# A layer stack on one core: the input ratio joined to the output matrix, state-space preparation dealt out anew, and a feed-forward entry with an early split and no wait at the barrier

## The chip, the cores and the metric

The kernel runs on one core of a Trainium2 chip. The core has TensorE (PE, matrix products into PSUM), VectorE (DVE), ScalarE (ACT), GpSimd (POOL) and SyncE (SP, which here only issues DMAs). The metric is the device time of one launch, in microseconds; the kernel before has a median of 1590.62 us over 3 runs.

## The reference

Three layers over 256 tokens of width 1024, all in float32. What matters here is the end of the first mixer, the feed-forward after it, and the mixer of the second layer:

```python
h = gdn_mixer(...)                                   # layer 0: gated delta rule, ends in o @ w_out
x = layer_norm(ALPHA * x + h, ln_g[0, 0], ln_b[0, 0])
f = (silu(x @ w1) * (x @ w3)) @ w2                   # D_FF = 2816
x = layer_norm(ALPHA * x + f, ln_g[0, 1], ln_b[0, 1])
# layer 1: s5_mixer, a diagonal complex state-space model, 64 groups of 16 channels and 64 states
u = x @ w_in
a_bar = exp(lam * dt)
b_bar = ((a_bar - 1.0) / lam)[..., None] * (b_re + 1j * b_im)
h_t = a_bar * h_(t-1) + einsum('gpc,tgc->tgp', b_bar, u_t)
y_t = einsum('gcp,tgp->tgc', c_re + 1j * c_im, h_t).real
# ... skip, gelu, gated output, layer norm, a mixture of experts; then a second block
# (convolution and gating mixer, a hierarchical mixture of experts, an embedding gate, a norm)
```

The factor (a_bar - 1) / lam is what is called the ratio below. It depends on group and state, not on time or channel.

## The kernel before

The program is one stream per engine, written out by hand, with counting semaphores between the streams. The weights go through a ring of three units of 16 KB per partition (`ring`); SyncE loads unit u once unit u - 3 is `released`.

**Split products.** A float32 product is made of three passes in a rounded type (`fp32r`): ScalarE rounds a weight piece of 128 x 1024 into a buffer (the high part), VectorE subtracts it from the ring in place (the low part), and TensorE runs high x high, low x high and high x low. The activations have a high part (`xT_r`) and a low part (`xl`) too.

**Feed-forward** (`ffn_tensor`, `ffn_scalar`, `ffn_vector`). The 22 chunks of hidden width are handled in blocks of 4, 4, 3, 4, 4, 3. Each chunk has a gate piece ("g"), an up piece ("u") and a down piece ("d"), 66 pieces in the order of `FF_ORDER`; in a block of four: g0 u0 g1 u1 g2 u2 d0 g3 u3 d1 d2 d3. A gate or up piece is 24 matmuls with 256 columns, a down piece 12 with 512. High parts go into three buffers in turn (`ff_high`), so ScalarE may round piece s once piece s - 3 has been used (`ffn_used`). ScalarE (L1247) and VectorE (L1304) walk through steps s = 0 to 70, one piece in each; silu, the product with the up half and the split of the hidden part follow some steps behind in the same loops (L1254, L1261; L1301, L1309). Gate units of the next block are loaded once the last gate piece of this block has been used, and so on for up and down.

**State-space preparation** (`s5_prepare`, called at the end of each VectorE step). It computes exp(lam dt), the ratio, b-bar, the powers of a_bar up to 3, a table of cosines and sines for 64 steps (`cosT`, `sinT`, by doubling in `turn` and `square`), and the output matrices `y_re[j]`, `y_im[j]` (C times a_bar to the j) from step 45 on. There are two layouts: `l2` (512 columns) and `st` (32 columns), together the 544 columns of `NP2`. ScalarE has the exponentials and sines, with a table load each time that the function set changes, and the masks that write the input matrices `bt`. `own_step` multiplies b-bar and y on TensorE after the feed-forward.

**The entry.** `gdn_tensor` ends with the output projection in four parts (`wout_ps` counts them). VectorE adds each to the residual and takes the row statistics, normalizes each half; TensorE turns it; ScalarE copies the turned half to `xT_r` (L421) and VectorE makes `xl` (`x_low`, L1095). At barrier 1 (`phase_end`) TensorE, ScalarE, VectorE and GpSimd each drain, add one to `phase_done` and wait for all four. SyncE also waits for that count before it issues the nine loads of the state-space parameters, which go over memory that the mixer used. `awake(n, b)` issues n products of the identity with itself whose result nobody reads. There are 10 behind the projection, 6 at the end of `turn_tensor` and 8 behind the barrier.

At the end of the feed-forward SyncE loads the next layer norm's row parameters into `lnp`, whose memory is two of the high buffers; VectorE's order there is: the last steps, the low parts of two pieces of the state-space input weights (`dn_low`, L282), the row sums (L1319 on), the norm (L355, L359).

Of the kernel before, what the change touches and what calls it, by code (L numbers as in the profile page):

```python
# [72 lines left out]
def program(nc, I, out, upto="all"):  # L73
    ctx = ExitStack()
    with ctx:
# [93 lines left out]
        k0_r = rounded("k0_r", K0_AT, D)  # L169
        o_split = rounded("o_split", 0, 2, DC, SEQ)  # L170
# [617 lines left out]
        def gdn_scalar(act):  # L788
# [352 lines left out]
        bbar_r, bbar_i = (work[:, WORK - (2 - i) * D:WORK - (1 - i) * D].rearrange("p (a b) -> p a b", a=PAIRS) for i in range(2))  # L1141
# [48 lines left out]
        def ff_buffer(s):  # L1190
            o = s5_in_high[:, 3, :] if s == FF_LAST else ff_high[s % 3]
# [48 lines left out]

        def ffn_scalar(act):
            for s in range(FF_PIECES + 5):
                if s < FF_PIECES:
# [19 lines left out]
                if s == 3:  # L1263
                    act.wait_ge(sem("s5_loaded"), 16 * LOADS_S5)
                    act.activation(dt, dt, ACT.Exp).then_inc(sem("s5_polar"), 1)
                for i, at_ in enumerate((26, 29, 33, 37)):
                    if at_ <= s < at_ + 2:
                        if s == at_:
                            act.wait_ge(sem("s5_drive"), i + 1)
                        t, plane = ((br_, bi_), (abr, abi))[i % 2][s - at_], 2 * (STEP - 1 - i) + s - at_  # L1270
# [24 lines left out]
        def ffn_vector(v):  # L1295
            for s in range(FF_PIECES + 5):
# [39 lines left out]
        def s5_prepare(v, s):  # L1336
# [10 lines left out]
            if s == 4:  # L1347
# [3 lines left out]
            if s == 5:  # L1351
                dve_link(v, v.tensor_scalar(kk_, th, 1.0 / TWO_PI, MAGIC, ALU.mult, ALU.add))
                dve_link(v, v.tensor_scalar(kk_, kk_, MAGIC, None, ALU.subtract))
                dve_link(v, v.scalar_tensor_tensor(th, kk_, -C1, th, ALU.mult, ALU.add))
            if s == 6:
                dve_link(v, v.scalar_tensor_tensor(th, kk_, -C2, th, ALU.mult, ALU.add))
                dve_link(v, v.scalar_tensor_tensor(th, kk_, -C3, th, ALU.mult, ALU.add))
                v.tensor_scalar(th, th, PI_LO, -PI_LO, ALU.min, ALU.max).then_inc(sem("s5_args"), 1)
# [8 lines left out]
            if s == 11:  # L1367
# [3 lines left out]
            if s == 12:  # L1371
                dve_link(v, v.tensor_tensor(t1[:, st], t0[:, st], t0[:, st], ALU.mult))
# [14 lines left out]
            if s == 14:  # L1387
                dve_link(v, v.tensor_scalar(t0, ar, 1.0, None, ALU.subtract))
                v.tensor_tensor(rho, t0, lam_re, ALU.mult)
                dve_link(v, v.tensor_tensor(t1, ai, lam_im, ALU.mult))  # L1390
            if s == 15:
                dve_link(v, v.tensor_tensor(rho, rho, t1, ALU.add))
                v.tensor_tensor(sn, ai, lam_re, ALU.mult)
                dve_link(v, v.tensor_tensor(t1, t0, lam_im, ALU.mult))
            if s == 16:
                dve_link(v, v.tensor_tensor(sn, sn, t1, ALU.subtract))
                v.tensor_tensor(rho, rho, kk_, ALU.mult)
                dve_link(v, v.tensor_tensor(sn, sn, kk_, ALU.mult))
# [2311 lines left out]
```

## Time and profile before

| | |
|---|---|
| median of 3 runs | 1590.62 us (1589.98 to 1591.07) |
| the profiled execution | 1593.2 us, span 1591.3 us |
| TensorE busy | 1508.8 us, 95% of the span |
| VectorE busy | 1019.4 us, 64% |
| ScalarE busy | 696.2 us, 44% |
| DMA | 443.45 MB, mean 279 GB/s |

The profile shows one execution. The span is what the records cover; the profiled run's own time is 1.9 us more. Matmuls overlap in TensorE's pipeline and their ends are modelled, so a matmul of 256 columns that is listed at 283 ns may be followed by the next after 120 ns. The granted clock is given as a share of TensorE's full 2.4 GHz; half is 1.2 GHz. All stretches below are in microseconds from the start of the span.

### The profile page before, as it was taken

The numbers are of one execution on the slowest core, as the hardware profiler recorded it, in microseconds if no ns is written. First come the engines' busy times: TensorE is split into PE (matmuls) and PEld (weight loads), VectorE is DVE, ScalarE is ACT, GpSimd is POOL, SyncE is SP. The second block draws the span as 40 slices with busy tenths as digits, with TensorE's granted clock in tenths as the row PEclk, the third lists the DMA queues.
The fourth block names the chain that finished last, engine by engine and source line by source line (L and its number), as shares of the span: only waits on it lengthen the run. The fifth ranks groups of instructions, "written<-read, shape, count | busy, mean of one in ns | idle before, by whom it ended". The sixth has DMA issues, their size and how long they took to land.

```text
span 1591.3 us, 24618 instructions
## 1 busy us (share of the span) xinstructions
PE 1508.8 (95%) x10552; PEld 1132.9 (71%) x10552; DVE 1019.4 (64%) x1446; ACT 696.2 (44%) x915; POOL 34.8 (2%) x34
## 2 busy tenths in 40 slices
PE   7999898999998999999999998999999999999986
PEld 7988778888997888888888887986434434443435
DVE  5776778999869688889888987785121121212127
ACT  5673335454443467667677675353101101110114
POOL 0000100000020000000000001000000000000001
PEclk9999999999999989999999999999999999999998
DMA  8431044344631449889989897378999999999981
GB/s 342 159 148 56 2 157 182 133 159 159 242 117 58 183 175 363 332 329 351 352 336 336 325 367 302 126 314 361 426 427 428 428 428 428 428 427 427 428 366 40
DMA packets 37841, 443.45 MB, mean 279 GB/s; under 512 B 5600, under 2 KB 6112, under 8 KB 10464
## 3 DMA queue, kind: packets, MB, share of 16 engines
q1 hardware_dynamic: 36576, 438.35, 68.9%
q10 hardware_dynamic: 1152, 3.46, 0.6%
q8 instruction: 87, 1.43, 0.4%
q14 instruction: 26, 0.21, 0.0%
HBM read 440.75 MB, written 1.05 MB: 278 GB/s over the span
## 4 chain that ended last, share of the span: by engine, by line
PE 75%; DVE 13%; DMA 7%; ACT 2%; issue 2%; SPq 0%; PEldq 0%; PEld 0%; ACTq 0%; DVEq 0%
PE psum L232 73%; DMA sb_spare<-moe_up 3%; DVE sb_ring_r L1304 2%; DMA sb_ring<-moe_wide 1%; DMA sb_ring<-ffn_wide 1%; DVE sb_split L2027 1%; DVE sb_work L2738 1%; DMA sb_lnp<-ln_rows 1%; PE psum L2534 1%; PE psum L2082 1%; DMA sb_work<-b_im 0%; DVE sb_work L1334 0%; DVE sb_ring_r L509 0%; DVE sb_work L1333 0%; DVE sb_work L1332 0%
## 5 line engine op out<-in xcount | busy, mean ns | idle before, releaser
L2027 DVE TENSOR_TENSOR sb_split<-sb_ring,sb_split 128x2048 fp32r<-128x2048 f32 (+1 forms) x144 | 301.1, 2110 | 44.8 <-ACT sb_split L2021 43.8
L232 PE MATMUL psum<-sb_work 64*64 64x64 f32 (+11 forms) x3392 | 285.9, 335 | 19.0 <-DVE sb_work L2738 7.8
L2021 ACT ACTIVATE sb_split<-sb_ring 128x2048 fp32r<-128x2048 f32 (+1 forms) x144 | 253.2, 1773 | 89.2 <-PE psum L232 60.6
L232 PE MATMUL psum<-sb_split 128*128 128x512 f32 (+1 forms) x912 | 268.7, 384 | 0.2 <-DVE sb_split L2341 0.2
L232 PEld LDWEIGHTS psum<-sb_work 128*64 128x64 f32 (+4 forms) x3392 | 148.6, 143 | 140.7 <-issue 119.5
L232 PE MATMUL psum<-sb_split,sb_lnp_r 128*128 128x512 f32 (+1 forms) x768 | 230.4, 374 | 1.4 <-DVE sb_split L2310 1.4
L232 PEld LDWEIGHTS psum<-sb_split 128*128 128x128 f32 x912 | 169.9, 188 | 30.7 <-DVE sb_split L2341 0.7
L232 PEld LDWEIGHTS psum<-sb_split,sb_lnp_r 128*128 128x128 f32 x768 | 142.7, 188 | 21.8 <-DVE sb_split L2310 1.6
L232 PE MATMUL psum<-sb_xT_r,sb_ring_r 128*128 128x256 f32 x512 | 144.3, 283 | 0.0
L2736 DVE TENSOR_TENSOR sb_work<-sb_work,psum 128x512 f32<-128x512 f32 x16 | 11.0, 689 | 169.4 <-ACT sb_work L2648 169.4
L2648 ACT ACTIVATE sb_work<-psum 128x512 f32<-128x512 f32 x16 | 9.6, 597 | 238.7 <-PE psum L232 238.7
L232 PE MATMUL psum<-sb_ring,sb_work 128*64 128x512 f32 (+1 forms) x448 | 104.7, 599 | 7.2 <-DVE sb_work L2738 4.7
L2706 DVE SCALAR_TENSOR_TENSOR sb_out_even<-psum,sb_work,sb_out_even 128x512 fp32r<-128x512 f32 x32 | 22.6, 747 | 130.4 <-ACT sb_out_even L2634 130.4
L232 PEld LDWEIGHTS psum<-sb_xT_r,sb_ring_r 128*128 128x128 f32 x512 | 98.2, 192 | 0.2
L232 PEld LDWEIGHTS psum<-sb_ring,sb_work 128*64 128x64 f32 (+1 forms) x448 | 33.7, 140 | 71.2 <-issue 63.4
L232 PE MATMUL psum<-sb_s_in_high,sb_gw_r 128*128 128x256 f32 x384 | 72.1, 289 | 11.5 <-DVE sb_ring_r L509 11.5
L2634 ACT ACTIVATE sb_out_even<-psum,sb_work 128x512 fp32r<-128x512 f32 x32 | 20.3, 684 | 136.4 <-PE psum L232 136.4
L232 PEld LDWEIGHTS psum<-sb_s_in_high,sb_gw_r 128*128 128x128 f32 x384 | 61.5, 195 | 13.1 <-DVE sb_ring_r L509 11.5
L232 PE MATMUL psum<-sb_xT_r,sb_lnp_r 128*128 128x256 f32 x224 | 64.1, 286 | 2.8 <-DVE sb_ring_r L1304 2.7
L232 PE MATMUL psum<-sb_ffn_r,sb_lnp_r 128*128 128x256 f32 x224 | 63.4, 283 | 0.0
L1304 DVE TENSOR_TENSOR sb_ring_r<-sb_ring,sb_lnp_r 128x1024 fp32r<-128x1024 f32 x43 | 52.5, 1224 | 16.0 <-ACT sb_lnp_r L1247 15.4
L2713 DVE TENSOR_TENSOR sb_xres<-sb_xres,psum 128x512 f32<-128x512 f32 x64 | 39.7, 682 | 30.7 <-PE psum L232 30.7
(468 smaller groups left out, 2677.7 us busy)
## 6 DMA issues: line engine op xcount, KB each, us to landing
sb_ring<-moe_wide SPq DMA_DIRECT2D x48, 2048.0 KB, 8.8
sb_work<-moe_up SPq DMA_DIRECT2D x33, 2048.0 KB, 25.2
sb_ring<-w_dense SPq DMA_DIRECT2D x23, 2048.0 KB, 8.5
sb_ring<-moe_last SPq DMA_DIRECT2D x24, 1536.0 KB, 8.3
sb_ring<-moe_up SPq DMA_DIRECT2D x18, 2048.0 KB, 25.1
sb_work<-moe_down SPq DMA_DIRECT2D x17, 2048.0 KB, 24.4
sb_ring<-ffn_wide SPq DMA_DIRECT2D x12, 2048.0 KB, 7.8
sb_ring<-moe_down SPq DMA_DIRECT2D x9, 2048.0 KB, 25.5
```

The lines of the kernel that those rows point to most:

```text
L232: return nc.tensor.matmul(o, lhsT, rhs, start=start, stop=stop, **kw)
L1304: v.tensor_tensor(ff_piece(ring_r, s), ff_piece(ring, s), ff_buffer(s).bitcast(F32), ALU.subtract)\
L2021: act.activation(wh[half_home(e, i)][:, 0:half_size(i)], half_raw(e, i), ACT.Copy).then_inc(sem("m1_high"), 1)
L2027: v.tensor_tensor(wl[home][:, 0:half_size(i)], half_raw(e, i), wh[home][:, 0:half_size(i)].bitcast(F32), ALU.subtract).then_inc(sem("m1_sp ...
L2082: ins = pe.transpose(o[:, c * P:(c + 1) * P], e_hid[:, c * P:(c + 1) * P], ident)
L2534: ins = pe.transpose(bank[2][:, c * P:(c + 1) * P], e_hid[:, c * P:(c + 1) * P], ident)
L2634: act.activation(out_even[:, 0, 512 * i:512 * i + 512], bank[4 + i][:, :], ACT.Copy, scale=gate_slot[:, (g - 1) % 2:(g - 1) % 2 + 1]).then ...
L2648: act.activation(e_silu[0], bank[0][:, :], ACT.Silu).then_inc(step, 1)
L2706: v.scalar_tensor_tensor(out_even[:, 1, d], bank[4 + i][:, :], gate_slot[:, (g - 1) % 2:(g - 1) % 2 + 1], out_even[:, 0, d].bitcast(F32), ...
L2713: v.tensor_tensor(xs, xs, combine_bank(i), ALU.add).then_inc(step, 1)
L2736: v.tensor_tensor(e_hid, e_silu[0], bank[1][:, :], ALU.mult).then_inc(step, 1)
L2738: v.tensor_copy(e_hidT[:, :, :], bank3(2)).then_inc(step, 1)
```

## The change

1. **The ratio goes to the output matrix.** b-bar is no longer formed. B is masked into `bt` and used by `own_step` as it was loaded, and `y_re[0]`, `y_im[0]` become C times the ratio. The ratio is then needed in the 32-column layout alone, and the squares, reciprocal and products that led to it run on 32 columns instead of 544. Tiles move with it: C is loaded beside `m1`, `b1_re` and `b1_im` lie at the end of `work`, `br_` and `bi_` are gone.
2. **The preparation is dealt to other steps**: the exponentials two steps later, the two halves of a power two steps apart, the last four turns in every second step (42 to 48), the chain of y from step 49 to 66 instead of 45 to 62.
3. **Piece 0 is split early.** ScalarE rounds it between the square root of the first half's norm and the copy of the first turned half, once `wout_ps` is 3, into a buffer of its own (`ff_first`); VectorE makes its low part after `x_low(0)`. TensorE runs the 16 matmuls on high x first and waits for `xl_ready` only before the other 8.
4. **No wait at barrier 1 for TensorE, ScalarE and VectorE**: `phase_left` drains and counts, and doesn't wait. The 6 and 8 `awake` products around the barrier go. GpSimd and SyncE still wait.

```diff
@@ barrier and entry
+        ff_first = rounded("ff_first", FFN_R_AT - D, D)
+        def phase_left(eng, n):
+            eng.drain().then_inc(sem("phase_done"), 1)
@@ turn_tensor
             if n in (0, 1):
-                if n == 0:
-                    awake(6, 4)
-                pe.wait_ge(sem("xl_ready"), 4 * (n + 1))
+                if n == 1:
+                    pe.wait_ge(sem("xl_ready"), 4 * (n + 1))
@@ gdn_scalar
                 norm_root(act, 0, h)
+                if h == 0:
+                    ff_first_high(act)
                 turn_half_evacuate(act, 0, None, xT_r, h)
@@ gdn_vector
                     if h == 1 and j == 1:
                         x_low(0)
+                        ff_low(v, 0)
@@ ffn_tensor
+            pe.wait_ge(sem("ffn_split"), 1)
+            wh_, wl_, o = ff_buffer(0), ff_piece(ring_r, 0), bank[4][:, 0:SEQ]
+            for k in range(DC):
+                mm(o, wh_[:, k, :], xT_r[:, k, :], k == 0, False)
+                mm(o, wl_[:, k, :], xT_r[:, k, :], False, False)
+            pe.wait_ge(sem("xl_ready"), 4)
+            for k in range(DC):
+                ins = mm(o, wh_[:, k, :], xl[:, k, :], False, k == DC - 1)
+            ins.then_inc(sem("ffn_used"), 1)
@@ new
+        def ff_first_high(act):
+            unit_ready(act, ff_unit(0))
+            act.wait_ge(sem("wout_ps"), 3)
+            act.activation(ff_buffer(0), ff_piece(ring, 0), ACT.Copy).then_inc(sem("ffn_high"), 1)
+        def ff_low(v, s):
+            v.wait_ge(sem("ffn_high"), s + 1)
+            v.tensor_tensor(ff_piece(ring_r, s), ff_piece(ring, s), ff_buffer(s).bitcast(F32), ALU.subtract)\
+             .then_inc(sem("ffn_split"), 1)
@@ ffn_scalar
-                    if s >= 3:
+                    if s >= 4:
                         act.wait_ge(sem("ffn_used"), s - 2)
-                if s == 3:
+                if s == 5:
                     act.wait_ge(sem("s5_loaded"), 16 * LOADS_S5)
                     act.activation(dt, dt, ACT.Exp).then_inc(sem("s5_polar"), 1)
-                for i, at_ in enumerate((26, 29, 33, 37)):
+                for i, at_ in enumerate((22, 28, 32, 36)):
...
-                if s == 6:
+                if s == 7:
                     act.wait_ge(sem("s5_args"), 1)
...
-                if s == 8:
+                if s == 11:
                     act.wait_ge(sem("s5_args"), 2)
@@ s5_prepare
-            if s == 7:
-                dve_link(v, v.tensor_tensor(kk_, lam_re, lam_re, ALU.mult))
-                dve_link(v, v.tensor_tensor(t1, lam_im, lam_im, ALU.mult))
-                dve_link(v, v.tensor_tensor(kk_, kk_, t1, ALU.add))
-            if s == 8:
-                dve_link(v, v.reciprocal(kk_, kk_))
             if s == 10:
-                v.tensor_scalar(y_im[0], y_im[0], -1.0, None, ALU.mult)
+                v.tensor_tensor(kk_[:, st], lam_re[:, st], lam_re[:, st], ALU.mult)
...
+                dve_link(v, v.reciprocal(kk_[:, st], kk_[:, st]))
...
-            if s == 17:
-                v.tensor_tensor(bbar_r, b1_re[:, :, :], st1(rho), ALU.mult)
...
+            if s == 19:
+                v.tensor_tensor(y_re[0], c_re[:, :, :], st1(rho), ALU.mult)
...
-            if s == 22:
-                half_product(v, br_[:, :, :], b2_re[:, :, :], rows2(rho), b2_im[:, :, :], rows2(sn), m2[:, :, :], ALU.subtract)
-            if s == 23:
-                half_product(v, bi_[:, :, :], b2_re[:, :, :], rows2(sn), b2_im[:, :, :], rows2(rho), m2[:, :, :], ALU.add)
...
-                if s == at_ + 1:
+                if s == at_ + 2:
                     half_product(v, n_i[:, :, :], p_r[:, :, :], rows2(ai), p_i[:, :, :], rows2(ar), m2[:, :, :], ALU.add)
...
-            if 45 <= s < 45 + 6 * (STEP - 1):
-                j, part = divmod(s - 45, 6)
+            if 49 <= s < 49 + 6 * (STEP - 1):
+                j, part = divmod(s - 49, 6)
...
-                if s == 41 + i:
+                if s == 42 + 2 * i:
                     turn(32, 16 * (i // 2), 16 * (i // 2) + 16, i % 2)
@@ the four streams (tensor; scalar and vector alike)
-            phase_end(pe, 1)
-            awake(8, 4)
+            phase_left(pe, 1)
```

## Rows read from the trace of the kernel before

**Rows 1.** The page, part 4: shares of the chain by line.
```profile
PE psum L232 73%; DMA sb_spare<-moe_up 3%; DVE sb_ring_r L1304 2%; DMA sb_ring<-moe_wide 1%; DMA sb_ring<-ffn_wide 1%; DVE sb_split L2027 1%; DVE sb_work L2738 1%; DMA sb_lnp<-ln_rows 1%; PE psum L2534 1%; PE psum L2082 1%; DMA sb_work<-b_im 0%; DVE sb_work L1334 0%; DVE sb_ring_r L509 0%; DVE sb_work L1333 0%; DVE sb_work L1332 0%
```

**Rows 2.** Windows: length, busy PE, PEld, DVE, ACT, POOL, PEclk, DMA share, GB/s.
```profile
233.58:309.51 75.93, 70.31 (x484) 64.16 (x482) 65.67 (x95) 38.05 (x50) 0.00 (x0) 1.00 0.43 165
309.51:375.27 65.76, 62.28 (x420) 55.88 (x420) 62.83 (x122) 34.41 (x50) 0.00 (x0) 1.00 0.47 184
375.27:434.88 59.61, 59.61 (x420) 55.99 (x421) 54.20 (x58) 29.71 (x38) 0.00 (x0) 1.00 0.47 179
```

**Rows 3.** The chain in order of time: start us, us, what.
```profile
262.99 8.62 DMA sb_ring<-ffn_wide
...
309.51 17.55 PE psum L232 x144
327.07 10.01 DMA sb_ring<-ffn_wide
...
338.26 1.22 DVE sb_ring_r L1304
...
373.99 1.24 DVE sb_ring_r L1304
375.27 54.25 PE psum L232 x396
```

**Rows 4.** Waits from 228 to 440: us in total, times, longest us.
```profile
PEld psum L232 <- DVE sb_ring_r L1304: 14.9, 19, 2.1
...
PE psum L232 <- DVE sb_ring_r L1304: 6.5, 12, 1.9
```

**Rows 5.** Timeline around barrier 1: start us, us, engine, line, instruction [idle before it].
```profile
227.34 0.60 ACT L421 ACTIVATE sb_xT_r<-psum 128x512 fp32r<-128x512 f32 x1 [0.32 <-PE psum L392]
227.97 0.69 DVE L1095 TENSOR_TENSOR sb_ffn_r<-psum,sb_xT_r 128x512 fp32r<-128x512 f32 x1 [0.23 <-ACT sb_xT_r L421]
...
227.99 5.84 PE L232 MATMUL psum<-sb_consts 128*128 128x128 f32 x28 [0.69 <-ACT sb_xT_r L421]
...
233.58 0.36 PE L232 MATMUL psum<-sb_xT_r,sb_lnp_r 128*128 128x256 f32 x1
```

**Rows 6.** Timeline from 214 to 222, where piece 0 would be split.
```profile
214.95 6.69 SPq L3314 DMA_DIRECT2D sb_ring<-ffn_wide  x2
...
218.12 1.09 ACT L421 ACTIVATE sb_xT_r<-psum 128x512 fp32r<-128x512 f32 x2 [4.30 <-PE psum L392]
...
221.32 0.69 DVE L1102 SCALAR_TENSOR_TENSOR sb_xres<-sb_xres,psum 128x512 f32<-128x512 f32 x1 [1.28 <-PE psum L232]
```

**Rows 7.** Windows, columns as in rows 2: the slow stretch at the entry.
```profile
225.40:232.20 6.80, 5.92 (x25) 5.03 (x26) 2.18 (x5) 2.42 (x4) 1.03 (x4) 0.53 0.40 155
```

**Rows 8.** Timelines of ScalarE and TensorE: the wait for the state-space loads, and behind it.
```profile
243.61 0.66 ACT L1265 ACTIVATE sb_work<-sb_work 128x544 f32<-128x544 f32 x1 [2.32 <-DMA sb_work<-b_im]
...
246.53 0.39 PE L232 MATMUL psum<-sb_xT_r,sb_lnp_r 128*128 128x256 f32 x1 [1.20 <-DVE sb_ring_r L1304]
```

**Rows 9.** Groups by form in the feed-forward: xcount | busy us, mean ns | idle.
```profile
L1332 DVE TENSOR_TENSOR sb_work<-sb_work 128x512 f32<-128x512 f32 x14 | 9.6, 684 | 0.0
...
L1364 DVE RECIPROCAL sb_work<-sb_work 128x544 f32<-128x544 f32 x1 | 3.5, 3545 | 0.0
...
L1366 DVE TENSOR_SCALAR sb_work<-sb_work 128x1024 f32<-128x1024 f32 x1 | 0.7, 687 | 0.0
...
L1389 DVE TENSOR_TENSOR sb_work<-sb_work 128x544 f32<-128x544 f32 x1 | 0.7, 725 | 0.0
...
L1450 DVE TENSOR_TENSOR sb_work<-sb_work 128x32 f32<-128x32 f32 x5 | 1.0, 193 | 0.2
...
L1272 ACT ACTIVATE sb_work<-sb_work,sb_front 128x512 f32<-128x512 f32 x16 | 10.6, 710 | 0.0
```

**Rows 10.** Timeline of VectorE at the end of the feed-forward.
```profile
432.27 0.69 DVE L1319 SCALAR_TENSOR_TENSOR sb_xres<-sb_xres,psum 128x512 f32<-128x512 f32 x1 [0.27 <-PE psum L232]
...
439.59 1.42 DVE L355 SCALAR_TENSOR_TENSOR sb_xres<-sb_xres,sb_small,sb_lnp 128x512 f32<-128x512 f32 x2 [0.70 <-DMA sb_lnp<-ln_rows]
```

More of the change, by code:

```diff
@@ L1140, in program @@
         assert fp.at == K0_AT
-        bbar_r, bbar_i = (work[:, WORK - (2 - i) * D:WORK - (1 - i) * D].rearrange("p (a b) -> p a b", a=PAIRS) for i in range(2))
+        b1_re, b1_im = (work[:, WORK - (2 - i) * D:WORK - (1 - i) * D].rearrange("p (a b) -> p a b", a=PAIRS) for i in range(2))
         assert K0_AT + D <= WORK - 2 * D
@@ L1146, in program @@
         cc_ = Carver(work, s5_phase_at, s5_phase_at + 2 * PAIRS * NSTEP)
-        b1_re, b1_im, m1 = cc_(PAIRS, 32), cc_(PAIRS, 32), cc_(PAIRS, 32)
+        c_re, c_im, m1 = cc_(PAIRS, 32), cc_(PAIRS, 32), cc_(PAIRS, 32)
         cc_ = Carver(work, y_at + 4 * D, y_at + 2 * STEP * D)
-        b2_re, b2_im, br_, bi_, m2, abr, abi = (cc_(DC, S5_STATE) for _ in range(7))
+        b2_re, b2_im, m2, abr, abi = (cc_(DC, S5_STATE) for _ in range(5))
         fr = Carver(ffn_r, 0, 3 * D + 2 * SEQ)
@@ L1370, in s5_prepare @@
                 dve_link(v, v.tensor_scalar(t0, t0, -2.0, 1.0, ALU.mult, ALU.add))
-            if s == 12:
-                dve_link(v, v.tensor_tensor(t1[:, st], t0[:, st], t0[:, st], ALU.mult))
+            if s == 14:
+                v.tensor_tensor(ar, rho, t0, ALU.mult)
+                dve_link(v, v.tensor_tensor(ai, rho, sn, ALU.mult))
+            if s == 15:
+                v.tensor_tensor(t1[:, st], t0[:, st], t0[:, st], ALU.mult)
                 dve_link(v, v.tensor_tensor(rot_r, sn[:, st], sn[:, st], ALU.mult))
@@ L1376, in s5_prepare @@
                 dve_link(v, v.tensor_scalar(rot_i, t1[:, st], 2.0, None, ALU.mult))
-            if s == 13:
-                v.tensor_tensor(ar, rho, t0, ALU.mult)
-                v.tensor_tensor(ai, rho, sn, ALU.mult)
+            if s == 16:
                 dve_link(v, v.tensor_tensor(decay4, rho[:, st], rho[:, st], ALU.mult))
@@ L1386, in s5_prepare @@
                 dve_link(v, v.tensor_tensor(decay4, decay4, decay4, ALU.mult))
[L1387 to L1398, printed above, removed]
-            if s == 17:
-                v.tensor_tensor(bbar_r, b1_re[:, :, :], st1(rho), ALU.mult)
-            if s == 18:
-                dve_link(v, v.tensor_tensor(m1[:, :, :], b1_im[:, :, :], st1(sn), ALU.mult))
+            if s == 17:
+                dve_link(v, v.tensor_scalar(t0[:, st], ar[:, st], 1.0, None, ALU.subtract))
+                v.tensor_tensor(rho[:, st], t0[:, st], lam_re[:, st], ALU.mult)
+                dve_link(v, v.tensor_tensor(t1[:, st], ai[:, st], lam_im[:, st], ALU.mult))
+                dve_link(v, v.tensor_tensor(rho[:, st], rho[:, st], t1[:, st], ALU.add))
+                v.tensor_tensor(rho[:, st], rho[:, st], kk_[:, st], ALU.mult)
@@ L1403, in s5_prepare @@
+            if s == 18:
+                v.tensor_tensor(sn[:, st], ai[:, st], lam_re[:, st], ALU.mult)
+                dve_link(v, v.tensor_tensor(t1[:, st], t0[:, st], lam_im[:, st], ALU.mult))
+                dve_link(v, v.tensor_tensor(sn[:, st], t1[:, st], sn[:, st], ALU.subtract))
+                dve_link(v, v.tensor_tensor(sn[:, st], sn[:, st], kk_[:, st], ALU.mult))
+                v.tensor_copy(t1[:, st], rot_i).then_inc(sem("s5_drive"), 1)
             if s == 19:
-                dve_link(v, v.tensor_tensor(bbar_r, bbar_r, m1[:, :, :], ALU.subtract))
@@ L1405, in s5_prepare @@
-                v.tensor_tensor(bbar_i, b1_re[:, :, :], st1(sn), ALU.mult)
+                v.tensor_tensor(y_re[0], c_re[:, :, :], st1(rho), ALU.mult)
             if s == 20:
-                dve_link(v, v.tensor_tensor(m1[:, :, :], b1_im[:, :, :], st1(rho), ALU.mult))
+                dve_link(v, v.tensor_tensor(m1[:, :, :], c_im[:, :, :], st1(sn), ALU.mult))
             if s == 21:
-                dve_link(v, v.tensor_tensor(bbar_i, bbar_i, m1[:, :, :], ALU.add))
+                dve_link(v, v.tensor_tensor(y_re[0], y_re[0], m1[:, :, :], ALU.add))
@@ L1410, in s5_prepare @@
             if s == 22:
-                half_product(v, br_[:, :, :], b2_re[:, :, :], rows2(rho), b2_im[:, :, :], rows2(sn), m2[:, :, :], ALU.subtract)
+                v.tensor_tensor(y_im[0], c_re[:, :, :], st1(sn), ALU.mult)
             if s == 23:
-                half_product(v, bi_[:, :, :], b2_re[:, :, :], rows2(sn), b2_im[:, :, :], rows2(rho), m2[:, :, :], ALU.add)
-                v.tensor_copy(cosT[:, :, 1:2], rot_r.unsqueeze(2)).then_inc(sem("s5_drive"), 1)
+                dve_link(v, v.tensor_tensor(m1[:, :, :], c_im[:, :, :], st1(rho), ALU.mult))
@@ L1462, in turn @@
                     half_product(v, sinT[:, i, o], cosT[:, i, a], p_i, sinT[:, i, a], p_r, tmp, ALU.add)
-            for at_, m in ((27, 2), (31, 4), (35, 8)):
+            for at_, m in ((28, 2), (32, 4), (36, 8)):
                 if s == at_:
@@ L1525, in own_step @@
             for q in range(DC):
-                for part, b in enumerate((bbar_r, bbar_i)):
+                for part, b in enumerate((b1_re, b1_im)):
                     for i in range(PQ):
@@ L3371, in _ @@
                         sp.wait_ge(sem("phase_done"), phase(1))
-                        for name, dst in (("lam_re", lam_re), ("lam_im", lam_im), ("log_dt", dt), ("c_re", y_re[0]), ("c_im", y_im[0]),
+                        for name, dst in (("lam_re", lam_re), ("lam_im", lam_im), ("log_dt", dt), ("c_re", c_re), ("c_im", c_im),
                                           ("b1_re", b1_re), ("b1_im", b1_im), ("b2_re", b2_re), ("b2_im", b2_im)):
@@ L3528, in _ @@
             gdn_vector(v)
-            phase_end(v, 1)
+            phase_left(v, 1)
             if LAST >= 2:
```

48 lines of the change are left out of this document (28 added, 20 removed).

## The prediction

> **What bounds the kernel now.** I read the chain that ended last first: TensorE's matmuls have 73% of the span, and the dearest VectorE line on it is the low part of the feed-forward's weight split (L1304, 2%) [rows 1]. So time is to be had where TensorE waits. Next I cut the stretch that the change touches into three and compared like with like [rows 2]. The feed-forward is 66 pieces: 44 gate or up pieces of 24 matmuls and 22 down pieces of 12. Counted back from the last one, piece 45 begins at 375.27 us (its low part, 1.24 us from 373.99, is the link before it), and piece 24 at 309.51 us [rows 3]. From 375.27 to 434.88 us TensorE is never idle: 14 gate or up and 7 down pieces take 59.61 us. The 21 pieces before them, the same mix, take 65.76, so 6.2 us are lost. The first 24 (16 and 8, the same mix again) want 59.61 x 24 / 21 = 68.1 us and take 75.93: 7.8 lost. Together **14.0 us**. (Gate and up matmuls start 17.55 / 144 = 0.12 us apart [rows 3], a piece of 24 takes 2.9 us; a down piece is left with 2.7.) The busy column shows only 5.6 + 3.5 of it, since short waits vanish under the modelled ends of matmuls.
>
> What is waited for is L1304, 21.4 us over the two TensorE rows (weight-load and matmul waits overlap, so they name the cause and not the size) [rows 4]. In the middle third VectorE is busy 62.83 of 65.76 us [rows 2]. VectorE is the bound there, through the state-space preparation dealt into the same steps.
>
> Third, the entry. TensorE waits for ScalarE's copy of x, runs filler matmuls from 227.99 us, drains, meets the barrier, runs filler again, and starts piece 0 only at 233.58, since the split of piece 0 begins behind the barrier [rows 5].
>
> **Entry.** The high part of piece 0 moves to ScalarE after wait 3 of the output projection, met at 214.95 us (SyncE's load issue waits for the same count [rows 6]). ScalarE has nothing from there to the copy at 218.12, and the rounding takes 1.05 us: hidden by 2 us. The low part goes on VectorE between x_low(0) and the last projection sum, which had 1.28 us of idle [rows 6]; the low part takes 1.22. It fits with nothing to spare; I allow 0.1 us on the layer norm. If that cover went, all 1.2 us would be on the path.
>
> TensorE can then start once its copy of x is there (227.34 + 0.60 = 227.94 us [rows 5]) and its drain is through: 228.1. The first 16 matmuls need only high x; the last 8 need the low part, done at 228.66, long before. But the clock: the granted clock is 0.53 from 225.4 to 232.2, that is 1.2 GHz, though TensorE was busy for 5.92 of these 6.80 us [rows 7]; it fell after a pause of TensorE of 2 us, which stays, and rose again some 4.2 us into unbroken work. The filler used to pay for that; now piece 0 does. If it rises at 232.25 again, matmuls 0.24 us apart (twice 0.12, as no row shows this kind at 1.2 GHz) make 17 by then and the other 7 take 0.8: piece 0 ends at 233.1 against 233.58 + 2.9 = 236.5. Gain **3.4 us**. Bounds: 5.5 us if the clock were full at once, 1.3 us if it rose another 4.2 us later (half of these 4.2 us are lost). Piece 1 is ready when asked: ScalarE 228.1 to 229.15, VectorE to 230.4.
>
> The Trainium skill, "TensorE: Matmul & The Clock Gate", The HAM clock gate, speaks against trusting the 3.4: the clock monitor runs on its own time, so how many matmuls meet the low clock differs from run to run. By it the entry lies anywhere between the bounds, in old and new kernel alike; our rows are one execution and can't show the spread.
>
> SyncE's nine state-space loads wait for the count of the drains. It comes 2 us sooner (drains at about 228.9), so the last, landing at 243.6 us, comes by 241.5. The exponential waits for them at step 5 and no more at 3, and step 5's own silu holds ScalarE until about 242: the 2.32 us wait goes, and with it TensorE's 1.20 us at 246.53 [rows 8]. ScalarE's table loads are as many as before. New behind it: VectorE blocks at step 5 for the exponential (about 244.2), and the low part of piece 6 stands behind it, due at 247.6. By hand: exponential 244.2, two products 245.6, mult 246.0, low part 247.2. It fits by 0.4 us. Steps 8 and 9 miss by some 0.2 each. I put 0.5 us.
>
> **Joining the ratio.** Off VectorE [rows 9]: the reciprocal over 544 columns, 3.55 us, becomes one over 32 (as the 32-wide rows, 0.2); three 544-wide products at 0.72 become 0.19 each (1.6 saved); nine at steps 14 to 16 become ten small ones (6.2 to 1.9); the negation (0.69) goes; six 512-wide at 0.68 (two products of br and bi, 4.1) go. The six 1024-wide for b-bar become six for the output matrix, of one kind and price. Small copies add 0.5. Sum: 3.35 + 1.6 + 4.3 + 0.7 + 4.1 - 0.5 = **13.6 us** of VectorE time.
>
> What that gives back is bounded by the 14.0 us. In the first 24 pieces VectorE's steps now cost (1.15 for the low part back to back, 0.75 for a hidden part's two instructions in every third step, and preparation) 3.4 us at most, at step 8, and mostly under 2.9: lost only the 0.5 above, and near nothing at step 13 (up weights asked at 262.99, landed 8.62 us later [rows 3]; with 2.4 us for the split that is 11.0, just what three down pieces and a gate piece between take). In steps 24 to 44 the work is 2.8 us less (two of the four last turns, 2.0 us each as three of the 512-wide instructions, move to steps 46 and 48; small copies worth 1.2 come in), and VectorE enters with its full lead: three buffers let it be 3.3 us ahead (two pieces, 5.7 us, less the 2.4 of a split), where it entered with none. 6.2 - 2.8 - 3.3 = 0.1; my running tally of steps 25 to 42 peaks at 4.1 against 3.3, so 0.8. I take **1.0 us**. ScalarE's masks at steps 28, 32 and 36 now wait for a count that VectorE raises only one step before: two masks of 0.71 [rows 9] and a rounding of 1.05 us make 2.5 us, beside 2.9 us or more that VectorE itself has in such a step, so they are hidden while VectorE is loaded; uncovered, they would cost up to 0.7 us each. Last, the boundary at piece 34: up weights asked at 327.07, there 10.01 us later, split by 338.26 + 1.22 = 339.48, 12.4 us in all, against 11.1 us of pieces [rows 3]. Old losses hid this; now it costs **1.3 us**.
>
> Remaining loss 0.5 + 1.0 + 1.3 = 2.8, so the feed-forward gives 14.0 - 2.8 = **11.2 us**. Bounds: 14.0 (nothing left) and 7.3 (the middle third's 6.2 stays whole, its load wait inside it).
>
> **Later.** The chain of y goes on to step 66, four steps longer. In steps 49 to 66 VectorE needs 1.2 + 1.2 + 0.25 = 2.65 us of 2.83. But steps 65 and 66 now put two 1024-wide products (1.15 us each, back to back) ahead of the two D_S5IN roundings and the layer norm's sums, on an engine that works in order. The sums began at 432.27 us, 0.27 after VectorE was free, and the norm began at 439.59, 0.70 after they were done, held by its row parameters [rows 10]. So the sums slip by 2.3 - 0.27 = 2.0 us and the norm by 2.0 - 0.7 = **1.3 us**; 0 if the parameters come later by as much, 2.0 if they come sooner. Those loads are set by TensorE's pieces and shift with it. All behind is ordered by the same counts and shifts along.
>
> **Sum.** 3.4 + 11.2 - 0.1 - 1.3 = 13.2 us. The profiled execution took 1593.2 us (span 1591.3 and 1.9 around it), 2.6 above the median of 1590.62; taken from the median: **1577.4 us**.
>
> **Rivals.** (a) *VectorE stays the bound of the middle third*: its 6.2 stays, for its steps are still over 3 us from 25 to 42. Gain 3.4 + 7.3 - 1.4 = 9.3: 1581.3. For: a tally above the lead. Against: 62.83 busy us with the entry lead at zero is what made the loss. Chance 0.17.
> (b) *The weight loads become the bound*: each of the three boundaries with 2 MB loads costs 1.3 to 2. Gain 13.2 - 2.7 = 10.5: 1580.1. For: 10.01 us at one. Against: 8.62 and faster at the others. Chance 0.12.
> (c) *The move to the entry doesn't do what it says* (clock late, or ScalarE and VectorE behind the drain): gain 13.2 - 3.4 = 9.8: 1580.8. Chance 0.08.
> (d) *Everything is given*, and the two end products are hidden: 5.5 + 14.0 - 0.1 = 19.4: 1571.2; half way, 1574.3. Chance 0.09.
> (e) *Slower*: without filler TensorE stays at 1.2 GHz through the first pieces, since each short wait for VectorE keeps it low. A piece at 1.2 GHz costs 2.84 more on the mean; the gain is gone after 27 us of it, and two blocks (24 pieces, 68 us more) would give 1577.4 + 68 = 1645, one block (12 pieces, 34 us) 1611. For: the fillers go at the very place where the clock is low. Against: it rose at 232 us with unbroken work, and the waits now get fewer. Chance 0.03.
>
> The forecast itself has 0.47, from 1574.5 to 1580. The range that leaves out no more than 2 in 10: **1573.0 to 1581.5**. A gain under 0.2% (3.2 us, about what a measurement can tell from no change) takes (a), (b) and (c) together: 0.04. So faster 0.93, same 0.04, slower 0.03.
>
> **What would show it.** Piece 0 starting near 228.1 and the clock up by 233; piece 45 starting 14 to 17 us sooner; from there to the last matmul 59.6 us as before; TensorE's waits for L1304 down from 21.4 to under 8 us; the idle at piece 34 for DMA; the layer norm after the feed-forward late or not against its parameters. Wrong would be: VectorE still over 95% busy between pieces 24 and 45, or a low clock past 236 us.

## The result, and the profile after

The median fell from 1590.7 us (6 runs, 1589.24 to 1591.6) to 1581.38 us (6 runs, 1578.4 to 1585.51): ratio 0.9944, 95% interval 0.9929 to 0.996. The gain is 9.3 us where 13.2 was forecast. Against the 1590.62 us that the forecast started from, the ratio gives 1581.7, just above the range's end of 1581.5. The direction was right and the size was not.

First the chain of the changed kernel, its shares by line, to hold against [rows 1].
```profile
PE psum L237 79%; DMA sb_spare<-moe_up 3%; DMA sb_ring<-ffn_wide 2%; DVE sb_ring_r L1268 1%; DVE sb_work L2764 1%; PE psum L2108 1%; PE psum L2560 1%; DVE sb_ring_r L513 0%; DVE sb_work L1787 0%; DVE sb_work L2762 0%; DMA sb_front<-conv_w 0%; ACT sb_work L2674 0%; DVE sb_ring_r L287 0%; PE psum L397 0%; ACT sb_lnp_r L1277 0%
```
TensorE went from 73 to 79% of the chain and VectorE's weight split from 2 to 1%. The load of the feed-forward weights went the other way, from 1 to 2%. These are shares of the whole span and price nothing, but they say where to look for the missing microseconds.

Next the windows of the changed kernel, with the columns and the cuts of [rows 2] (piece 0, piece 24, piece 45, last matmul).
```profile
231.92:303.70 71.78, 70.81 (x481) 66.51 (x482) 53.01 (x85) 42.02 (x54) 4.02 (x7) 0.97 0.48 181
303.70:367.33 63.63, 61.10 (x422) 55.93 (x421) 59.15 (x117) 32.51 (x47) 0.00 (x0) 1.00 0.49 191
367.33:428.61 61.28, 59.99 (x421) 55.98 (x419) 55.68 (x61) 29.77 (x38) 0.00 (x0) 1.00 0.46 174
```
The thirds took 75.93, 65.76 and 59.61 us before. The first two gave 4.2 and 2.1 us, and the last, which had no loss, is 1.7 us longer. VectorE has 12.7 us less work in the first third and 3.7 less in the second: the arithmetic taken off it is gone as forecast, and less of it than hoped came back as time.

In the first window piece 0 carries the slow clock (0.97 on the mean). So I cut anew for every kernel: from the start of the last transposes of x to piece 2; the feed-forward from piece 2 to piece 65; from there to the first state-space matmul; the rest. (The last two down pieces are run in two halves, so piece 65 starts half way into piece 64.) "Loss" is what the second stretch takes above its pace, 2.875 us for each gate or up piece and 2.742 for each down piece, read where TensorE never waits.

| us | before | after | change | forecast |
|---|---|---|---|---|
| transposes to piece 2 | 13.89 | 10.51 | -3.38 | -3.4 |
| piece 2 to piece 65 (loss) | 191.30 (14.3) | 184.52 (7.6) | -6.78 | -11.2 |
| piece 65 to the state space | 15.92 | 17.28 | +1.36 | +1.4 (norm 1.3, low part at the entry 0.1) |
| the three | 221.11 | 212.31 | -8.8 | -13.2 |

What lies outside is the same work: in this profiled execution the part ahead ran 3.9 us later and the part behind was 4.7 us shorter. Most of it goes with the clock: ahead of the entry it was recorded at 1.2 GHz for 10.2 us instead of 3.4, behind the state space's start for some 41 instead of 48, and half of such time is lost.

Where the 7.6 us of loss sit: pieces 5 and 8, 0.57; piece 13, 1.0; piece 34, 2.34; pieces 35 to 43, 1.8; piece 46, 1.67. Pieces 13, 34 and 46 are each the first up piece behind a pair of 2 MB loads. Here are ScalarE's roundings of these three, in the timeline of the changed kernel.
```profile
270.13 1.06 ACT L1277 ACTIVATE sb_lnp_r<-sb_ring 128x1024 fp32r<-128x1024 f32 x1 [3.81 <-DMA sb_ring<-ffn_wide]
...
331.92 1.06 ACT L1277 ACTIVATE sb_lnp_r<-sb_ring 128x1024 fp32r<-128x1024 f32 x1 [2.60 <-DMA sb_ring<-ffn_wide]
...
369.19 1.06 ACT L1277 ACTIVATE sb_lnp_r<-sb_ring 128x1024 fp32r<-128x1024 f32 x1 [5.09 <-DMA sb_ring<-ffn_wide]
```
And the windows, columns as in [rows 2], from SyncE's issue of the *gate* load of each pair (its queue has them at 257.25, 318.27 and 355.58 us) to the landing of the up load.
```profile
257.25:270.13 12.88, 12.71 (x72) 11.23 (x73) 8.39 (x15) 6.32 (x10) 0.00 (x0) 1.00 0.91 342
318.27:331.92 13.65, 13.59 (x80) 11.57 (x79) 12.70 (x27) 6.64 (x11) 0.00 (x0) 1.00 0.88 335
355.58:369.19 13.61, 13.25 (x76) 11.55 (x77) 10.79 (x19) 4.33 (x6) 0.00 (x0) 1.00 0.88 328
```
The same three windows of the kernel before:
```profile
259.24:271.61 12.37, 9.88 (x54) 8.50 (x55) 12.13 (x17) 5.63 (x8) 0.00 (x0) 1.00 0.86 341
324.19:337.10 12.91, 11.85 (x64) 9.69 (x63) 12.46 (x27) 6.41 (x11) 0.00 (x0) 1.00 0.81 326
362.10:375.62 13.52, 12.27 (x63) 9.51 (x62) 13.24 (x19) 3.76 (x6) 0.00 (x0) 1.00 0.78 312
```
The two loads of 2 MB, issued 2.9 to 3.8 us apart, need 12.4 to 13.7 us in either kernel, with the DMA engines 78 to 91% busy. (A down load of 2 MB, which has the engines nearly to itself, lands after 7.5 to 7.7 us.) Before, VectorE was busy 12.13 of 12.37 us and 13.24 of 13.52 beside them: TensorE was late for VectorE anyway, and the load hid behind that. Once VectorE is on time, the pair is what is late. At piece 34 VectorE is still busy for 12.70 of 13.65 us, so these windows alone don't decide between the two there; the experiments on the loads below do.

The Trainium skill, "DMA: Bandwidth & Descriptors", Bandwidth, gives 341 GB/s for a transfer of 1 MB and 425 for 16 MB, measured with transfers issued from GpSimd, by which the 4.19 MB of a pair would take an estimated 9.9 to 12.3 us. The rows show 312 to 342 GB/s over the whole of it and 12.4 to 13.7 us; the measurement decides.

The chain of the changed kernel (start us, us, what) runs through the load at piece 13, where the forecast said "near nothing":
```profile
257.42 3.15 PE psum L237 x24
...
260.58 9.52 DMA sb_ring<-ffn_wide
...
270.13 1.07 ACT sb_lnp_r L1277
...
271.22 1.24 DVE sb_ring_r L1268
...
272.50 2.53 PE psum L237 x19
```
Waits of the changed kernel from 228 to 434 us, as in [rows 4]:
```profile
ACT sb_lnp_r L1277 <- DMA sb_ring<-ffn_wide: 13.1, 6, 5.1
...
PEld psum L237 <- DVE sb_ring_r L1268: 7.4, 10, 1.9
...
PE psum L237 <- DVE sb_ring_r L1268: 4.7, 7, 1.7
```
TensorE's two rows fell from 21.4 to 12.1 us. They still name VectorE's low part, since that is the last step before the matmul; ScalarE's row shows what was late ahead of it. The kernel before had this row too, shorter, and with under 0.5 us of loss at each of the three boundaries, since VectorE was behind anyway:
```profile
ACT sb_lnp_r L1247 <- DMA sb_ring<-ffn_wide: 8.2, 3, 3.7
```

### The profile page after: what moved, and what is told of

It is laid out like the page before. It is cut to its first block, busy times and chain, and to the rows that moved or that the text cites. A ratio compares the mean times of both kernels' runs of the same rounds, so it can differ in the third digit from the quotient of the medians.

```text
span 1581.7 us, 24553 instructions
## 1 busy us (share of the span) xinstructions
PE 1502.2 (95%) x10524; PEld 1129.6 (71%) x10524; DVE 1005.7 (64%) x1441; ACT 697.2 (44%) x915; POOL 36.4 (2%) x34
## 4 chain that ended last, share of the span: by engine, by line
PE 81%; DVE 9%; DMA 5%; ACT 2%; issue 2%; PEldq 0%; ACTq 0%; DVEq 0%; PEld 0%
PE psum L237 79%; DMA sb_spare<-moe_up 3%; DMA sb_ring<-ffn_wide 2%; DVE sb_ring_r L1268 1%; DVE sb_work L2764 1%; PE psum L2108 1%; PE psum L2560 1%; DVE sb_ring_r L513 0%; DVE sb_work L1787 0%; DVE sb_work L2762 0%; DMA sb_front<-conv_w 0%; ACT sb_work L2674 0%; DVE sb_ring_r L287 0%; PE psum L397 0%; ACT sb_lnp_r L1277 0%
## 5 line engine op out<-in xcount | busy, mean ns | idle before, releaser
L2674 ACT ACTIVATE sb_work<-psum 128x512 f32<-128x512 f32 x16 | 9.6, 597 | 236.8 <-PE psum L237 236.8
L1268 DVE TENSOR_TENSOR sb_ring_r<-sb_ring,sb_lnp_r 128x1024 fp32r<-128x1024 f32 x42 | 51.5, 1225 | 14.8 <-ACT sb_lnp_r L1277 14.3
```

The costliest lines, as they stand in the source:

```text
L2674: act.activation(e_silu[0], bank[0][:, :], ACT.Silu).then_inc(step, 1)
```

## Experiments

Ratios are to the kernel before on the same chip, as recorded; they are not the quotient of the medians and can differ from it by up to 0.0008. Its medians were 1590.99, 1590.71 and 1590.66 us in the three groups of runs.

**The two halves alone.** The entry without the preparation:
```diff
  kernel before, and of the change only:
+ ScalarE rounds piece 0 after wait 3 of the output projection, VectorE makes its low part before the last sum;
+ TensorE takes high x first
- the wait at barrier 1 on TensorE, ScalarE and VectorE, and the filler around it
```


> The kernel before with the entry alone (early split of piece 0, high x first, no wait at barrier 1, no filler around it); preparation as before. My account of the changed kernel (entry 3.4 us, preparation 6.8, tail 1.4 back): gain 3.3 to 4.5 us, about 1587, and the 14 us of losses between pieces 2 and 45 stay within 1.5. Rival, the two halves need each other (an earlier entry is eaten by VectorE, which is the bound behind it): gain under 1.5 us.

Measured: 1590.66 us, ratio 0.9997 (0.9982 to 1.0012). The entry itself does what it should (10.38 us to piece 2, against 13.89), and the feed-forward takes it back. Its timelines:
```profile
243.18 0.66 ACT L1295 ACTIVATE sb_work<-sb_work 128x544 f32<-128x544 f32 x1 [4.52 <-DMA sb_work<-b_im]
```
```profile
246.09 0.39 PE L237 MATMUL psum<-sb_xT_r,sb_lnp_r 128*128 128x256 f32 x1 [3.40 <-DVE sb_ring_r L1268]
```
The old preparation asks for the exponential at step 3. With TensorE 3 us earlier, ScalarE gets there earlier and waits 4.52 us for the same loads instead of 2.32 [rows 8]; TensorE stands 3.40 us, and a low clock follows (0.5 from 247.2 us on). My 3.3 to 4.5 us for this kernel overlooked it.

The preparation without the entry:
```diff
  kernel after, but
+ the wait at barrier 1 on all three engines, and filler before and behind it, as before
- the early split of piece 0, and high x first
```


> The changed kernel with the old entry: the ratio in the output matrix and the new dealing of the preparation alone. My account: 6.8 us off between pieces 2 and 65, 1.3 us back at the layer norm, so a gain of 5 to 6 us, about 1585.2; loads at the boundaries of pieces 13, 34 and 46 still cost 1 to 2.3 us each. Rival (halves need each other): the sum of this gain and that of the entry alone differs from the whole by over 2 us.

Measured: 1586.0 us, 0.9969 (0.9951 to 0.9986), a gain of 4.9 us. Its profile has 14.08 us to piece 2 and 184.43 in the feed-forward: all of the preparation's 6.9, none of the entry's. (A low clock behind 439.5 us makes its third stretch 19.0.) Its losses at pieces 13, 34 and 46 are 1.3, 1.9 and 1.6 us, so they don't hang on the early entry.

The halves alone give 0.3 and 4.9 us, together 9.3. To see whether the step of the exponential is what joins them, I gave the entry alone later steps:
```diff
  e1, and
- exponentials at steps 3 and 6, sines at 8; VectorE's preparation at steps 4 to 8 and 11
+ exponentials at steps 5 and 7, sines at 11; VectorE's preparation at steps 5 to 9 and 12
```


> The kernel before with the entry, and of the new dealing only this: the wait for the state-space loads and the first exponential at step 5 instead of 3, the second at 7, the sines at 11, and VectorE's steps 4 to 8 and 11 one later. The entry alone gained nothing, since ScalarE stood at step 3 for the loads until 243.2 us whatever TensorE did. If that wait is the reason: the loss of 5.1 us around pieces 2 to 4 falls under 1.5, gain 3 to 4.5 us against the kernel before, about 1587. Rival, VectorE eats it (the 544-wide products and the 3.5 us reciprocal behind): the loss moves to pieces 5 to 10 and the gain is under 1.5 us.

Measured: 1586.8 us, 0.9973 (0.9952 to 0.9994), a gain of 3.9 us, and no loss in pieces 2 to 4. ScalarE doesn't wait for the loads any more:
```profile
244.32 1.28 ACT L1295 ACT_TABLE_LOAD   x1
245.61 0.66 ACT L1295 ACTIVATE sb_work<-sb_work 128x544 f32<-128x544 f32 x1
```
The rest of its feed-forward loses 15.2 us, as the old preparation does. So the entry's 3.4 us come through only with the later exponential, which in the full change the other half brings.

**The loads.** More bytes in the same place:
```diff
  kernel after, and ahead of the gate loads of blocks 1 and 3 on SyncE
+ if u in (U_FFN + 3, U_FFN + 9):
+     sp.dma_start(spare[:, at:at + 1536], I["w_dense"][0][:, 0:1536])     # 0.75 MB
  (ScalarE waits for these two at step 55, long after they have landed)
```


> The changed kernel with 0.75 MB that nobody uses loaded just ahead of the gate unit of blocks 1 and 3 (pieces 12 and 33). Theory L, the weight loads are the bound at the block boundaries: at 0.4 MB per us they come 1.8 us later, the loss around piece 13 goes from 1.0 to about 2.8 us and around piece 34 from 2.3 to about 4.1 us. Theory V, VectorE is the bound there: no change, under 0.4 us at each.

Measured: 1586.78 us, 0.9973 (0.9958 to 0.9989), by the ratios 4.6 us over the changed kernel. Losses at the three boundaries 4.37, 5.8 and 3.71 us; each holds 1.7 us of a low clock that followed the stall (0.5 from 270.8, 335.6 and 373.2 us on), so 2.7, 4.1 and 2.0, against 1.0, 2.34 and 1.67. The windows from the issue of the added load to the landing, and ScalarE behind it:
```profile
252.65:267.45 14.80, 13.97 (x81) 12.13 (x82) 8.43 (x15) 6.32 (x10) 0.00 (x0) 1.00 0.94 379
```
```profile
267.45 1.06 ACT L1277 ACTIVATE sb_lnp_r<-sb_ring 128x1024 fp32r<-128x1024 f32 x1 [3.83 <-DMA sb_ring<-ffn_wide]
```
0.75 MB cost 1.7 and 1.8 us of TensorE's time where they were added, and 0.3 at piece 46, where nothing was. A load with slack would have swallowed them: there was none at piece 13 either.

Less work for VectorE:
```diff
  kernel after, steps 25 to 35
- half_product(v, n_r[:, :, :], p_r[:, :, :], rows2(ar), p_i[:, :, :], rows2(ai), m2[:, :, :], ALU.subtract)
+ v.memset(n_r[:, 0, 0:1], 0.0)
  (n_i alike: the kernel leaves out the powers of a_bar in the input matrices)
```


> The changed kernel without the six complex products of steps 25 to 35 (the powers of a_bar in the input matrices are left out; the counts stay), 12 us less for VectorE there. Theory L: losses around pieces 34 and 46 stay, 1.5 to 2.8 and 1.2 to 1.7 us, and only the 1.8 us between them (pieces 35 to 43) go. Theory V: all 5.8 us between pieces 32 and 47 go, under 0.5 us are left.

Measured: 1579.53 us, 0.9924 (0.9895 to 0.9954), from two runs. The loss of pieces 35 to 43, 1.8 us, is gone, and those at 13, 34 and 46 stay at 1.1, 2.5 and 2.6 us although VectorE is busy only 46.77 of the 64 us from 300 to 364. Its waits from 228 to 430:
```profile
ACT sb_lnp_r L1277 <- DMA sb_ring<-ffn_wide: 17.2, 6, 5.2
...
PEld psum L237 <- DVE sb_ring_r L1268: 6.7, 6, 2.4
```
So VectorE had 1.8 us and the loads nearly all of the rest. Taking the 1.8 us away gave back only 0.7 of it in this stretch (loss 6.9 instead of 7.6): the boundaries took the rest, that of piece 46 above all.

The wait itself taken away: the gate and up units are laid out by chunks and loaded in two parts, chunks 0 and 1 as soon as chunk 1 of the block before is used.
```diff
- act.wait_ge(unit loaded)
+ act.wait_ge(first half loaded) for chunks 0 and 1, then the unit
- load(u, ...) once the whole slot is free
+ for kind, h in (("g", 0), ("u", 0), ("g", 1), ("u", 1), ("d", 1)):
+     half_load(kind, b, h)        # columns 0:2D, then the rest; down units whole
```


> The changed kernel with gate and up units laid out chunk by chunk and loaded in two parts: chunks 0 and 1 as soon as the last block's chunk 1 has been used, the rest as before. Theory L: the losses around pieces 13, 34 and 46 (1.0, 2.3, 1.7 us) fall to under 0.3 each, gain 3.5 to 5 us, about 1577. Theory V: they stay, because VectorE's rounding is what is late, gain under 1 us.

Measured: 1576.65 us, 0.9914 (0.9895 to 0.9934), 4.7 us under the changed kernel. Nothing at pieces 13 and 46 and 0.37 at 34; 2.8 us of loss in all, in pieces 5 to 8 and 35 to 43, where VectorE's steps are long. Its chain, over the places where the changed kernel stood:
```profile
252.25 37.23 PE psum L237 x264
...
347.70 62.78 PE psum L237 x444
```
TensorE runs 264 and 444 matmuls without a link to another engine. (The layout of the weights changes along with the time of the loads; the run doesn't part the two.)

**The tail.** The preparation's two last steps put behind the layer norm (which runs between the second and the third D_S5IN low part):
```diff
- s5_prepare(v, s)
+ if s not in (65, 66):
+     s5_prepare(v, s)
  dn_low(v, D_S5IN + 2)
+ for s in (65, 66):
+     s5_prepare(v, s)
```


> The changed kernel with the last two products of the chain of y (steps 65 and 66) moved behind the layer norm. If they delay the norm, as I worked out (1.3 us): from the last matmul piece to the first state-space matmul 15.9 us instead of 17.3, gain 1.3 us against the changed kernel, about 1580. Rival: the row parameters' load sets the norm anyway: no gain.

Measured: 1581.08 us, 0.9944 (0.9925 to 0.9962), no difference in the median. The profile shows the microsecond: 16.22 us from piece 65 on instead of 17.28, and the norm waits for its parameters again, as in [rows 10].
```profile
433.20 1.41 DVE L360 SCALAR_TENSOR_TENSOR sb_xres<-sb_xres,sb_small,sb_lnp 128x512 f32<-128x512 f32 x2 [1.00 <-DMA sb_lnp<-ln_rows]
```

**Filler at the entry.** More of it, at the end of the stage before:
```diff
- awake(10, 4)
+ awake(18, 4)
```


> The changed kernel with 8 more filler products in the pause before the last transposes (18 instead of 10). If the low clock of the entry comes from that pause: the granted clock stays full from the transposes on, transposes 0.8 us sooner and piece 0 2 us sooner, gain 2.5 to 3 us, about 1578.5. [...]

Measured: 1580.31 us, 0.9933 (0.9912 to 0.9954). In its profile the clock stays at its upper level, 2.4 GHz, and the entry takes 7.90 us instead of 10.51. Windows at the same place: first this kernel,
```profile
229.00:235.00 6.00, 5.07 (x39) 4.60 (x40) 4.80 (x7) 4.92 (x6) 2.85 (x4) 1.00 0.75 281
```
then the changed kernel, at 1.2 GHz for most of it.
```profile
229.10:235.90 6.80, 5.75 (x26) 5.12 (x27) 5.17 (x7) 5.14 (x6) 3.00 (x5) 0.57 0.64 232
```
2.6 us in one execution each, and medians that hardly differ. So I ran it again:

> The changed kernel with 18 filler products instead of 10, once more, for the clock at the entry. Five of the traces with the early entry and no more filler show 10.5, 10.4, 10.5, 9.4 us (clock low there) and 7.9 us (clock full) from the last transposes to piece 2, so the full clock comes without filler too. If the filler holds the clock: 7.9 us again. If it is chance alone: 10.4 to 10.5 us in about half of such runs.

Measured: 1580.81 us, 0.9938 (0.9918 to 0.9959), 7.90 us.

**All of them.** Tail, filler and halves together:
```diff
  e5 + e6 + e7
```


> The last three together. If they are independent: gain 1.3 + 2.7 + 4.2 = 8.2 us against the changed kernel, about 1573. Rival: VectorE becomes the bound again once the loads are early and takes 2 us back: 1575.

Measured: 1574.4 us, 0.9904 (0.9886 to 0.9922), 7.0 us under the changed kernel where the three alone gave 0.3, 1.1 and 4.7. Its feed-forward loses 2.7 us, as that of e7, so VectorE takes nothing back there. Twice more, with the filler and without:

> The version with halves, tail and filler once more, beside the one without filler. Filler holds the clock: 7.9 us at the entry, and 1 to 2.5 us faster on the median than without filler. Chance alone: the two medians agree within 1 us.

Measured: 1575.34 us, 0.9896 (0.9862 to 0.9929); 7.91 us to piece 2.
```diff
  e5 + e7
```


> Halves and tail, without the filler. Filler holds the clock: sometimes 10.5 us at the entry, median near 1576. Chance alone: as with filler, near 1574.5.

Measured: 1574.72 us, 0.9896 (0.9862 to 0.9929); 10.46 us to piece 2, with this clock:
```profile
229.00:235.00 6.00, 5.26 (x25) 4.87 (x24) 4.76 (x5) 5.16 (x6) 3.49 (x5) 0.50 0.60 195
```
The clock was full at the entry in all four profiles with the longer filler. Without it, it was low in five (the changed kernel, e1, e5, e9, e12), full in two (e3, e7) and half way in one (e4, 9.40 us). The medians show no gain from it: 1575.34 with, 1574.72 without. The version to keep is e12, some 16 us under the kernel before and 7 under the changed one.

## Why the prediction missed

**The entry, 3.4 us: right, 3.38.** Piece 0's split was done early and hidden. In the changed kernel's timelines:
```profile
218.90 1.06 ACT L1263 ACTIVATE sb_ff_first<-sb_ring 128x1024 fp32r<-128x1024 f32 x1 [1.20 <-PE psum L237]
...
222.01 1.09 ACT L425 ACTIVATE sb_xT_r<-psum 128x512 fp32r<-128x512 f32 x2 [2.04 <-PE psum L397]
```
```profile
223.84 1.22 DVE L1268 TENSOR_TENSOR sb_ring_r<-sb_ring,sb_ff_first 128x1024 fp32r<-128x1024 f32 x1
225.21 0.69 DVE L1109 SCALAR_TENSOR_TENSOR sb_xres<-sb_xres,psum 128x512 f32<-128x512 f32 x1
```
```profile
229.41 1.78 PE L397 MATMUL psum<-sb_consts,sb_xres 128*128 128x128 f32 x8 [2.00 <-DVE sb_xres L364]
...
231.92 0.58 PE L237 MATMUL psum<-sb_xT_r,sb_ff_first 128*128 128x256 f32 x1 [0.74 <-ACT sb_xT_r L425]
```
The split leaves 2 us before the copy of x, the last sum starts without a wait, and piece 0 starts 2.5 us after the transposes do. The close agreement owes something to luck, for two values inside it were off and cancelled. The clock was low for 4.9 us of piece 0, not 4.15:
```profile
231.92:236.80 4.88, 4.88 (x23) 4.88 (x24) 4.35 (x4) 4.23 (x4) 3.90 (x6) 0.50 0.55 164
```
But matmuls at 1.2 GHz start 0.21 us apart (23 of them in these 4.88 us) and not 0.24. In the kernel before, too, the clock was low until 232.65 us, a little later than the 232.25 of the working. And had the clock been full, the gain would have been 6.0 us and not 5.5, by the 7.91 us of e3. The Trainium skill, "TensorE: Matmul & The Clock Gate", The HAM clock gate, says that how many matmuls run slow differs between runs of one kernel. The traces agree: kernels with the same instructions here took 7.91 us (e3) and 10.51 us (the changed kernel). Of rival (c) nothing came in the full change.

**The exponential at step 5, 0.5 us: right, 0.57.** e1 and e9 show that it also carries the entry: without it the feed-forward takes the 3.4 us back.

**VectorE's work in the middle, 1.0 us: half of it.** Pieces 35 to 43 lose 1.8 us, gone in e4. The tally of steps against the lead was some 0.8 too kind. Rival (a) wanted 6.2 us for the middle third, which loses 4.0 us, 2.3 of it for the load.

**The load boundaries, 1.3 us in all: this is the failed step.** The prediction counted "near nothing at step 13", 1.3 us at piece 34 and nothing at piece 46. The three cost 1.0, 2.34 and 1.67 us, 5.0 together. Three things went wrong.

Piece 46 was left out, since the last third of the kernel before had no loss. The trace had its price: by the prediction's own method (the time to landing, 2.4 us for the split, less 11.1 us of pieces) it is 10.6 + 2.4 - 11.1 = 1.9 us. Here are the issue of that up load and the rounding behind it, in the kernel before:
```profile
364.97 0.33 SPq L3314 DMA_DIRECT2D sb_ring<-ffn_wide  x1
...
375.62 1.06 ACT L1247 ACTIVATE sb_lnp_r<-sb_ring 128x1024 fp32r<-128x1024 f32 x1 [3.66 <-DMA sb_ring<-ffn_wide]
```
So rival (b)'s counterargument, "8.62 and faster at the others", was a misreading: the others took 10.0 and 10.6 us.

At piece 13 the up load was timed from its own issue, 262.99 us. But the gate load had been issued 3.8 us ahead of it, since TensorE was late between the two, and both use the same DMA engines. With TensorE on time the gap was 3.3 us and the up load took 9.5 us of its own. From the *gate's* issue the pair took 12.4 us before and 12.9 after. That the load had no slack stood in [rows 3]: it is a link of the chain that ended last, as the one at 327.07 us is. TensorE has one up piece, three down pieces and a gate piece to do meanwhile, 2.88 + 8.22 + 2.88 = 14.0 us. Against that stand the pair, 12.9 to 13.7 us in the changed kernel, and 2.4 us of split, so 15.3 to 16.1 us: 1.3 to 2.1 us at each of the three.

And at piece 34 the pair took 0.7 us longer than before, 13.65 instead of 12.91. No row of the kernel before showed that.

By e7 the loads cost 4.8 us (7.6 less 2.8), 3.5 more than forecast. With the 0.8 of VectorE that is the 4.4 us missed in the feed-forward, within 0.1. Rival (b) had the place and 1.3 to 2 for each; its chance of 0.12 leaned on that misreading. Its sum, 10.5 us of gain, lacked the 0.8 us of VectorE. The 9.3 us of rival (a) are the measured gain to the digit, but by chance: the middle third did not keep its 6.2 us.

**The layer norm, -1.3 us: right, -1.36.** Two products stand before its sums, and it doesn't wait for its parameters. Timeline of the changed kernel, against [rows 10]:
```profile
423.38 1.22 DVE L1470 TENSOR_TENSOR sb_work<-sb_work 128x1024 f32<-128x1024 f32 x1
424.63 1.23 DVE L1472 TENSOR_TENSOR sb_work<-sb_work 128x1024 f32<-128x1024 f32 x1
425.89 2.36 DVE L287 TENSOR_TENSOR sb_ring_r<-sb_ring,sb_s_in_high 128x1024 fp32r<-128x1024 f32 x2
428.17 0.68 DVE L1347 SCALAR_TENSOR_TENSOR sb_xres<-sb_xres,psum 128x512 f32<-128x512 f32 x1
```

**Its own signs.** Piece 45 came 7.9 us sooner, not 14 to 17 (3.9 of the difference lies before the change). TensorE's waits for the low part are 12.1 us, not under 8. The stretch from piece 45 on took 61.28 us, not 59.6: the third boundary, which the forecast never priced. Piece 0 started at 231.92 us and the clock was low until 236.8, past the 236 that was named as a sign of being wrong; less the 3.9 us both are where the forecast had them, 228.0 and 232.9. VectorE was busy for 59.15 of 63.63 us between pieces 24 and 45, 93%, just under the 95% named.

Left open: why a gain of about 2.6 us at the entry in the profiles with filler is not in the medians. The spread of single runs, some 4 us to either side, is larger than that.

## What to carry to other kernels

Where two loads are issued close together, time the second from the first one's issue, and ask whether the gap between them will stay. In this case the pair took 12.4 to 13.7 us with gaps of 2.9 to 3.8 us; other gaps were not tried. Price every place of the same kind, also one that shows no wait now. Before writing off a wait as "hidden", ask what hides it; if the change removes that very cover, put the full price in the sum. And test halves of a change with what they lean on: one alone may be worth nothing because the other moves the wait out of its way.

## What the runs showed of the hardware

The clock can be low in places where TensorE has no pause. In the changed kernel from 40 to 46 us (windows, columns as before), and what TensorE did ahead of it (timeline):
```profile
40.00:46.00 6.00, 6.00 (x40) 6.00 (x41) 1.80 (x3) 0.93 (x3) 0.00 (x0) 0.72 0.47 199
```
```profile
38.70 3.64 PE L237 MATMUL psum<-sb_front,sb_xT 128*128 128x16 f32 x32
```
TensorE is busy for all 6.00 us, and the granted clock is 0.72. The low stretch begins at 42.3 us, behind 32 products of only 16 columns without a gap. At the entry it began behind a pause of 2.0 us. That the narrow products are the reason is not shown: the kernel before ran the same 32 from 39.8 us and kept its clock.

Some of these stretches are in one profile and not in the other: the changed kernel has them at 42.3 and 172.0 us, and the kernel before has none ahead of 195. The spread of single runs goes with the clock: over the 63 runs of the kernel before in the three groups (sd 3.2 us) time and mean granted clock have a correlation of -0.72, some 1.0 us for each 0.001 of clock. So a term of 1 to 3 us is better read in the stages of the profiles than in medians of four to six runs.
